# Two transformer blocks on one core: the one-hot matrix OJ of the expert gates made by GpSimd instead of VectorE

## The chip, the cores and the metric

One of the eight cores of a Trainium2 chip runs the whole program. The metric is the device time of one execution in microseconds. The engines are TensorE (PE, the matmuls, with its weight loads PEld), VectorE (DVE), ScalarE (ACT), GpSimd (POOL) and SyncE (SP, which only issues DMAs here). Each has its own queue of instructions in order, and they are tied together by semaphores.

## What is computed

Two blocks on 256 tokens of width 2048, in float32. The first has stick-breaking and dilated attention and a convolutional feed-forward part; the second has a recurrent and a gating group, and then the part on which the change bears, a mixture over 16384 experts in 128 x 128 (`peer`):

```
q = (x @ w_q).reshape(B, S, 8, 2, 128)
s = einsum('bshpk,hpnk->bshpn', q, sub_keys)
top_s, top_i = top_k(s, 16)
cand_s = top_s[..., 0, :, None] + top_s[..., 1, None, :]
cand_i = top_i[..., 0, :, None] * 128 + top_i[..., 1, None, :]
best_s, pos = top_k(cand_s, 16)          # for each head
ids, g = cand_i[pos], softmax(best_s)
out[t] = sum over the token's 8 * 16 picks of gelu(x[t] . expert_u[id]) * g * expert_v[id]
```

So each token picks 128 experts (8 heads times 16), each with an index i = id / 128, an index j = id mod 128 and a weight g.

## The kernel before

All of the program is written out engine by engine, with hand-placed waits. Every matrix of weights comes as tiles of 1 MB into three buffers `raw` (line 254), in pieces of 128 x 512. ACT rounds two pieces at a time to `hiR` (line 266), DVE subtracts that from `raw` into `loR` (line 274, the "split"; nine of these in one stage are POOL's), and PE multiplies with both, so that the sum has nearly full precision. A ring of eight pieces lies between them, and ACT and DVE work four pieces ahead (`LA`). One step `s` is one piece.

For 224 of the 256 tokens (`TD`) the mixture is computed densely. The experts are taken in three ranges of the index i (43, 43 and 42). In each range, a stage U multiplies x by all expert rows of U (`wide`, lines 292 and 293; 4 steps for each i; the sum of the two halves on DVE in line 1349, gelu in line 1357, into `S_`), and a stage V multiplies the gated result by the rows of V (`experts_out`, lines 1406 and 1408). The remaining 32 tokens (`TS`) are done by gathering their rows of U and V: POOL issues an indirect DMA (line 1447) into two buffers `ring`, and DVE takes each row into a dot product (line 1469) or a sum (line 1476). `SLOT` gives the steps at which that happens: every ten steps in stages U of the ranges 1 and 2, and every 3.5 steps in the stages V.

During each stage U the gate matrix G[j, i, t] is made: the sum of the weights g of token t over picks with these j and i. Four tokens are one gate, 56 gates for 224 tokens, `gate_at` gives the step of each: every 2 steps in range 0, every 2.8 and 2.7 in ranges 1 and 2. With the 128 picks of a token on the partitions, DVE builds three tiles in f16, each in two buffers by the parity of the gate:

- OJ (128 x 4 x 128), one where the pick's j equals the column: in range 0 with the four tokens innermost (line 1286), in the other ranges with the tokens outermost (line 1290). Both read `selb[:, 1]` (the j of each pick, f16) and the iota table `ioh4`.
- OI (128 x 4 x ni), the same for i (line 1294).
- OG, OI times the high and the low half of g (line 1297).

PE multiplies OJ (stationary) with OG (moving), eight matmuls for each gate (line 1311), two steps behind DVE. ACT brings the result to `G_` one step later (line 1320). DVE's gate k waits until PE has done gate k - 2 (semaphore `g_mm`), PE waits for `g_og` (two increments a gate) and for the bank (`g_ev`). In stage U, DVE's order within a step is: split, choice of experts or sum of V, sum of U (line 1349), gate, gathered row. POOL's program in these stages holds the gathers alone (`pool_rows`), and `selb` is made ahead of range 0 by ACT (lines 1126 and 1127) and DVE (line 1262).

Of the kernel before, what the change touches and what calls it, by code (L numbers as in the profile page):

```python
# [7 lines left out]
F16 = mybir.dt.float16  # L8
# [4 lines left out]
D = 2048  # L13
T = 256
# [99 lines left out]
def build(nc, A, out):  # L114
# [86 lines left out]
    OI = [at(f"OI{i}", o + 2 + 0.375 * i, [128, 4, NI], F16) for i in range(2)]  # L201
    OG = [at(f"OG{i}", o + 2.75 + 0.6875 * i, [128, 2, 4, NI], F16) for i in range(2)]
    o = RB + 2 * SG + 4.125
    selb = at("selb", o, [128, 4, T], F16)
    ioh4 = at("ioh4", 73, [128, 128, 4], F16)
    hrep, vsum = at("hrep", o + 2.25, [128, D]), at("vsum", o + 2.25, [128, D])
    yT = [at("yT0", 8, [128, 8, TD]), at("yT1", o + 10.25, [128, 8, TD])]
    idx = at("idx", 15, [128, ROWS, 2], U32)
    gs = at("gs", 15.25, [128, ROWS])
    dots = at("dots", 15.375, [128, ROWS, 2])  # L210
# [108 lines left out]

    norm_tmp = [tmp0, tmp1, tmp2, tmp3]  # L320
    norm_gain = [gp, g2, g4, g5]
    norm_load = [("gp", 16), ("g2", 16), ("ffn_const", 32), ("g5", 16)]
    norm_to = [XA, XA, XB, XA]
    norm_rs = [st[:, 4:6], st[:, 36:38], st[:, 68:70], st[:, 100:102]]

# [49 lines left out]
    def pe_norm_first(e, i, b):  # L375
        pe_keep(e, i, 0, b)
        if i == 0:
            e.wait_ge(S("ident"), 16)
        for q in range(TURN_FIRST[i]):
            pe_norm_turn(e, i, q)  # L380
        pe_keep(e, i, 1, b)
# [722 lines left out]
    def act_choice(e, s):  # L1104
        c, d = divmod(s - 4, 4)
        if s in (4, 7):
            c, d = 0, 7 - s
        if d == 0 and 0 <= c < 16:
            e.wait_ge(S("piece"), P_Q + (4 * c + 4 if c else 7))
            e.copy(qT[c][:, :], bank[c % 4][:, 0:T]).then_inc(S("qT"), 1)  # L1110
        h, d = divmod(s - TK0, TKP)
        if d == 1 and 0 <= h < 8:
            for tb in range(2):
                e.wait_ge(S("tk_sc"), 2 * h + tb + 1)
                if h:
                    e.wait_ge(S("tk"), TKN * (h - 1) + 20)
                e.copy(sc[tb][:, :, :].rearrange("p a b -> p (a b)"), bank[4 + tb][:, 0:T]).then_inc(S("tk_cp"), 1)
        for n, tb in enumerate((1, 0)):
            d = s - (DEC0 + DECP * n)
            if d == 8:  # L1120
                e.wait_ge(S("dec"), ND * n + 25)
                e.activation(fl[6][:, :], fl[6][:, :], ACT.Exp).then_inc(S("d_exp"), 1)
            elif d == 14:
                e.wait_ge(S("d_tr"), n + 1)
                for i in range(2):
                    e.copy(selb[:, i, half(tb)], bank[4][:, i * 128:(i + 1) * 128]).then_inc(S("sel_g"), 1)
                e.mul(selb[:, 2, half(tb)], bank[4][:, 256:384], 4096.0).then_inc(S("sel_g"), 1)

    def dve_choice(e, s):
        lo8, hi8 = slice(0, 8), slice(8, 16)  # L1130
# [52 lines left out]
        for n, tb in enumerate((1, 0)):  # L1183
# [48 lines left out]
            elif d in (3, 6):  # L1232
                w = 14 if d == 3 else 21
                for i, m in enumerate((8, 4, 2, 1)):
                    e.wait_ge(S("dec"), ND * n + w - 1 + i)
                    to = eq[:, 0:m, :, :] if m > 1 else by_rank_out(I_ if d == 3 else J_)
                    e.tensor_tensor(to, eq[:, 0:m, :, :], eq[:, m:2 * m, :, :], ALU.add).then_inc(S("dec"), 1)
            elif d == 7:
                e.tensor_tensor(v2(e1), bv, bv[:, :, 0:1].to_broadcast([128, 8, 16]), ALU.subtract).then_inc(S("dec"), 1)
            elif d == 9:  # L1240
                e.wait_ge(S("d_exp"), n + 1)
                e.reduce_sum(sm, v2(e1), AX.X).then_inc(S("dec"), 1)
                e.wait_ge(S("dec"), ND * n + 26)
                e.reciprocal(rc, sm).then_inc(S("dec"), 1)
                e.wait_ge(S("dec"), ND * n + 27)
                e.tensor_tensor(v2(g_), v2(e1), rc.unsqueeze(2).to_broadcast([128, 8, 16]), ALU.mult).then_inc(S("dec"), 1)
            elif d == 10 and n == 0:
                own, ids = slice(TD - 128, 128), xi
                e.wait_ge(S("dec"), ND)
                e.scalar_tensor_tensor(ids[own, :], I_[own, :], 128.0, J_[own, :], ALU.mult, ALU.add).then_inc(  # L1250
                    S("sp_ix"), 1)
                e.wait_ge(S("sp_ix"), 1)
                e.tensor_scalar(ids[own, :], ids[own, :], 2.0, None, ALU.mult).then_inc(S("sp_ix"), 1)
                e.wait_ge(S("sp_ix"), 2)
                for j in range(128 // TS):
                    part, cs = slice(TS * j, TS * j + TS), slice(ROWS * j, ROWS * j + ROWS)
                    e.tensor_copy(idx[part, :, 0], ids[own, cs]).then_inc(S("sp_ix"), 1)
                    e.tensor_scalar(idx[part, :, 1], ids[own, cs], 1.0, None, ALU.add).then_inc(S("sp_ix"), 1)
                    e.tensor_copy(gs[part, :], g_[own, cs]).then_inc(S("sp_ix"), 1)
            elif d == 14:  # L1260
                e.wait_ge(S("sel_g"), 3 * n + 3)
                e.scalar_tensor_tensor(selb[:, 3, half(tb)], bank[4][:, 256:384], 4096.0, selb[:, 2, half(tb)],
                                       ALU.mult, ALU.subtract).then_inc(S("sel"), 1)


# [8 lines left out]
    def dve_gates(e, r, s):  # L1274
        i0, i1 = RANGES[r]
        ni = i1 - i0
        for n in gate_at(r, s):
# [4 lines left out]
                e.wait_ge(S("choice_const"), 48)  # L1282
            if k >= 2:
                e.wait_ge(S("g_mm"), k - 1)
            if r == 0:
                e.tensor_tensor(OJ[v][:, :].rearrange("p (a t) -> p a t", t=4),
                                selb[:, 1:2, ts].to_broadcast([128, 128, 4]), ioh4[:, :, :], ALU.is_equal).then_inc(
                    S("g_og"), 1)
            else:
                e.tensor_tensor(OJ[v][:, :].rearrange("p (t a) -> p t a", t=4),  # L1290
                                selb[:, 1, ts].unsqueeze(2).to_broadcast([128, 4, 128]),
                                ioh4[:, :, 0].unsqueeze(1).to_broadcast([128, 4, 128]), ALU.is_equal).then_inc(
                    S("g_og"), 1)
# [3 lines left out]
            e.tensor_tensor(OG[v][:, :, :, 0:ni], OI[v][:, None, :, 0:ni].to_broadcast([128, 2, 4, ni]),
                            selb[:, 2:4, ts].unsqueeze(3).to_broadcast([128, 2, 4, ni]), ALU.mult).then_inc(
                S("g_og"), 1)

    def pe_gates(e, r, s):
        ni = RANGES[r][1] - RANGES[r][0]
        for n in gate_at(r, s - 2):
            k, v, b = NG * r + n, n % 2, u_bank(r) + 2 + n % 2
            e.wait_ge(S("g_og"), 2 * k + 2)
            if n >= 2:
                e.wait_ge(S("g_ev"), k - 1)
            for j in range(4):
                of = slice(j, 512, 4) if r == 0 else slice(128 * j, 128 * j + 128)
                for w in range(2):  # L1310
                    m = e.matmul(bank[b][:, ni * j:ni * j + ni], OJ[v][:, of], OG[v][:, w, j, 0:ni], start=(w == 0),  # L1311
                                 stop=(w == 1))
# [137 lines left out]

    def act_rows(e, s):
        if SLOT.get(s - 1) == NROW:
            e.wait_ge(S("sp_dot"), 1)
            e.activation(gated[:, :], gated[:, :], ACT.Gelu_apprx_tanh).then_inc(S("sp_gelu"), 1)

    def dve_rows(e, s):
        if SLOT.get(s - 2) == NROW:
            e.wait_ge(S("sp_gelu"), 1)
            e.wait_ge(S("sp_ix"), 2 + 3 * (128 // TS))
            e.tensor_tensor(gated[:, :], gated[:, :], gs[:, :], ALU.mult).then_inc(S("sp_a"), 1)  # L1460
        m = row_of(s)
        if m is not None:
            e.wait_ge(S(f"row{m % 2}"), 16 * (m // 2 + 1))
# [5 lines left out]
                e.scalar_tensor_tensor(rg, rg, 1.0, hrep[:, cs], ALU.mult, ALU.mult,  # L1469
                                       accum_out=dots[:, j, m % 2:m % 2 + 1]).then_inc(S("sp_use"), 1)  # L1470
            elif j == 0:
                e.wait_ge(S("sp_a"), 1)
                e.tensor_scalar(vsum[:, cs], rg, gated[:, 0:1], None, ALU.mult).then_inc(S("sp_use"), 1)
            else:
                e.wait_ge(S("sp_use"), m - 1)
# [1 line left out]
                    S("sp_use"), 1)  # L1477
        if SLOT.get(s) == NROW:
            e.wait_ge(S("sp_use"), NROW)
            e.tensor_tensor(gated[:, :], dots[:, :, 0], dots[:, :, 1], ALU.add).then_inc(S("sp_dot"), 1)  # L1480

# [242 lines left out]
    def act_program(e):  # L1726
# [1 line left out]
        e.wait_ge(S("cst"), 2)  # L1728
        act_sqrt_table(e, 0)
        e.wait_ge(S("x0"), 16)  # L1730
        e.activation(tmp0[:, 0, :], x[:, 0, :], ACT.Square, accum_out=ss[:, 0:1]).then_inc(S("x0sq"), 1)
        e.wait_ge(S("x0sq"), 1)
        e.wait_ge(S("x1sq"), 1)
        act_root(e, 0, ss)
        act_norm_hi(e, 0, 0)
        split_hi(e, 0)
# [136 lines left out]
    def dve_program(e):  # L1873
# [3 lines left out]
        e.memset(warm[:, :], 0.0).then_inc(S("cst"), 1)  # L1877
        e.wait_ge(S("x1"), 16)
        e.scalar_tensor_tensor(tmp0[:, 1, :], x[:, 1, :], 1.0, x[:, 1, :], ALU.mult, ALU.mult,
                               accum_out=ss[:, 1:2]).then_inc(S("x1sq"), 1)  # L1880
        dve_root(e, 0, ss)
        dve_norm_scale(e, 0, 0)
        dve_norm_scale(e, 0, 1)
# [163 lines left out]
    def pool_program(e):  # L2047
# [207 lines left out]
```

## Time and profile before

| | |
|---|---|
| median of 3 runs | 2960.62 us (2955.79 to 2963.03) |
| the profiled execution | 2955.81 us, of which the span of instructions is 2954.5 us |
| mean granted clock of PE | 0.997 |
| PE busy | 2911.7 us (99%), 18502 matmuls |
| DVE busy | 2139.5 us (72%) |
| ACT busy | 1570.7 us (53%) |
| POOL busy | 419.0 us (14%), 304 instructions |
| splits on DVE (line 274) | 1255.0 us |
| read from memory | 623 MB, 212 GB/s over the span |

Busy shares are means over the whole span; which engine sets the pace has to be read stage by stage. A row of PE has a modelled end, so that matmuls overlap in the rows: the distance between starts says more than the duration. Idle time on an engine that is not the limit costs nothing.

### The profile page before, as it was taken

Reading aid. Unit: us, or ns where it says so; the run is one execution under the profiler, and the core shown is the slowest. Engines: PE = TensorE matmul, PEld = TensorE weight load, DVE = VectorE, ACT = ScalarE, POOL = GpSimd, SP = SyncE. Lnnn points to the kernel's source line nnn. Section 1 sums busy time; section 2 is a strip of 40 time slices with the busy share of each in tenths; the row PEclk is TensorE's granted clock in tenths of the full one; section 3 lists DMA queues with packets and bytes.
Section 4 is the critical chain, followed back from the end, with each engine's and each line's share of the span. In section 5 each row is a group of like instructions: output and inputs, shape, how many; then the busy total and the mean of one; then the engine's idle time right before and its main releaser. Section 6 shows DMA issues by size and latency. Waiting matters only on the chain.

```text
span 2954.5 us, 45739 instructions
## 1 busy us (share of the span) xinstructions
PE 2911.7 (99%) x18502; PEld 2631.0 (89%) x18502; DVE 2139.5 (72%) x3352; ACT 1570.7 (53%) x2406; POOL 419.0 (14%) x304
## 2 busy tenths in 40 slices
PE   9999999999999999999998999999999999999998
PEld 7888888888888888899898999999999999999997
DVE  5566566666666455676589889778999777999776
ACT  4467755555555443577444556444556444556534
POOL 0011101111111000143020000232010133110131
PEclk9999999999999999999999999999999999999999
DMA  7544445555556554654564555788666788666784
GB/s 259 177 151 152 156 177 186 185 186 187 185 186 222 190 198 143 221 177 170 208 211 171 190 183 203 270 302 298 230 236 227 247 306 302 234 232 239 272 310 168
DMA packets 99009, 631.53 MB, mean 214 GB/s; under 512 B 11376, under 2 KB 12784, under 8 KB 31216
## 3 DMA queue, kind: packets, MB, share of 16 engines
q1 hardware_dynamic: 80368, 561.49, 54.3%
q0 software_dynamic: 18432, 67.12, 6.3%
q8 instruction: 148, 2.42, 0.3%
q14 instruction: 61, 0.50, 0.0%
HBM read 623.32 MB, written 4.19 MB: 212 GB/s over the span
## 4 chain that ended last, share of the span: by engine, by line
PE 78%; DMA 9%; DVE 8%; ACT 3%; issue 2%; SPq 0%; ACTq 0%; DVEq 0%
PE ps L292 26%; PE ps L293 13%; PE ps L1406 6%; PE ps L314 6%; PE ps L316 6%; PE ps L315 6%; DMA ring<-in_u_rows_dram,idx 5%; DMA ring<-in_v_rows_dram,idx 4%; PE ps L1408 3%; DVE loR L274 3%; PE ps L305 2%; PE ps L304 2%; PE ps L303 2%; ACT hiR L266 1%; PE ps L1311 1%
## 5 line engine op out<-in xcount | busy, mean ns | idle before, releaser
L274 DVE TENSOR_TENSOR loR<-raw,hiR 128x1024 fp32r<-128x1024 f32 x1017 | 1255.0, 1241 | 621.9 <-ACT hiR L266 618.4
L266 ACT CAST hiR<-raw 128x1024 fp32r<-128x1024 f32 x1026 | 1074.4, 1051 | 803.3 <-PE ps L1408 324.3
L292 PE MATMUL ps<-XA,hiR 128*128 128x448 f32 (+1 forms) x3936 | 1343.9, 391 | 10.7 <-DVE loR L274 9.3
L293 PE MATMUL ps<-XA,loR 128*128 128x224 f32 (+1 forms) x3936 | 1069.3, 272 | 0.0
L292 PEld LDWEIGHTS ps<-XA,hiR 128*128 128x128 f32 x3936 | 739.7, 188 | 127.1 <-DVE loR L274 6.6
L293 PEld LDWEIGHTS ps<-XA,loR 128*128 128x128 f32 x3936 | 747.7, 190 | 0.6
L1406 PE MATMUL ps<-hl,hiR 128*128 128x448 f32 x2048 | 651.0, 377 | 6.2 <-DVE loR L274 5.9
L1408 PE MATMUL ps<-hl,loR 128*128 128x224 f32 x2048 | 543.5, 265 | 0.0
L1406 PEld LDWEIGHTS ps<-hl,hiR 128*128 128x128 f32 x2048 | 385.2, 188 | 42.8 <-DVE loR L274 9.2
L1408 PEld LDWEIGHTS ps<-hl,loR 128*128 128x128 f32 x2048 | 392.1, 191 | 0.2 <-issue 0.2
L1447 POOL DMA_INDIRECT ring<-in_u_rows_dram,idx x64 | 103.2, 1612 | 716.8 <-DVE ring L1469 664.8
L1320 ACT ACTIVATE G__147<-ps 128x172 f32<-128x172 f32 (+1 forms) x168 | 52.9, 315 | 227.8 <-PE ps L1311 227.7
L1447 POOL DMA_INDIRECT ring<-in_v_rows_dram,idx x64 | 105.2, 1644 | 407.9 <-DVE vsum L1476 391.8
L314 PE MATMUL ps<-hiR,Y 128*128 128x512 f32 x344 | 133.8, 389 | 0.0
L315 PE MATMUL ps<-loR,Y 128*128 128x512 f32 x344 | 133.8, 389 | 0.0
L316 PE MATMUL ps<-hiR,Y 128*128 128x512 f32 x344 | 133.8, 389 | 0.0
L1469 DVE SCALAR_TENSOR_TENSOR ring<-ring,hrep 128x1024 f32<-128x1024 f32 x64 | 78.2, 1222 | 54.6 <-DMA ring<-in_u_rows_dram,idx 54.5
L1476 DVE SCALAR_TENSOR_TENSOR vsum<-ring,gated,vsum 128x1024 f32<-128x1024 f32 x62 | 79.5, 1282 | 47.5 <-DMA ring<-in_v_rows_dram,idx 47.4
L303 PE MATMUL ps<-XB,hiR 128*128 128x256 f32 x384 | 110.0, 286 | 0.0
L305 PE MATMUL ps<-XB,loR 128*128 128x256 f32 x384 | 108.6, 283 | 0.0
L304 PE MATMUL ps<-XB,hiR 128*128 128x256 f32 x384 | 108.6, 283 | 0.0
L314 PE MATMUL ps<-hiR,XA 128*128 128x512 f32 x256 | 101.0, 394 | 2.3 <-DVE loR L274 1.8
(307 smaller groups left out, 3490.1 us busy)
## 6 DMA issues: line engine op xcount, KB each, us to landing
raw<-in_u_dram SPq DMA_DIRECT2D x128, 1024.0 KB
raw<-in_v_dram SPq DMA_DIRECT2D x128, 1024.0 KB
raw<-in_w_up_dram SPq DMA_DIRECT2D x86, 1024.0 KB
raw<-in_w_down_dram SPq DMA_DIRECT2D x43, 1024.0 KB
raw<-in_w_in_qk_dram SPq DMA_DIRECT2D x32, 1024.0 KB
raw<-in_w_out_dram SPq DMA_DIRECT2D x32, 1024.0 KB
raw<-in_w_in_dram SPq DMA_DIRECT2D x24, 1024.0 KB
raw<-in_w_in_v_dram SPq DMA_DIRECT2D x16, 1024.0 KB
```

The lines of the kernel that those rows point to most:

```text
L266: e.copy(hiR[:, r:r + 2, :], raw[n % NR][:, q:q + 2, :]).then_inc(S("hi"), 1)
L274: e.tensor_tensor(loR[:, r:r + 2, :], raw[n % NR][:, q:q + 2, :], hiR[:, r:r + 2, :].bitcast(F32), ALU.subtract).then_inc(S("lo_pool" if p ...
L292: e.matmul(both, wh, X.hl[:, :, k, 0:nt], start=(k == 0), stop=False, skip_group_check=True)
L293: m = e.matmul(dst[:, 0:nt], wl, X.h[:, k, 0:nt], start=False, stop=(k == KC - 1), skip_group_check=True)
L303: e.matmul(dst, wh, X.h[:, k, :], start=(k == 0), stop=False)
L304: e.matmul(dst, wh, X.l[:, k, :], start=False, stop=False)
L314: e.matmul(dsts[tb], ah_, hi, start=first, stop=False)
L315: e.matmul(dsts[tb], ah_, lo, start=False, stop=False)
L316: m = e.matmul(dsts[tb], al_, hi, start=False, stop=last)
L1406: e.matmul(b[:, 0:2 * TD].rearrange("p (a t) -> p a t", a=2), wh, hl[:, :, i, :], start=(i == 0), stop=False, skip_group_check=True)
L1408: m = e.matmul(b[:, 0:TD], wl, hl[:, 0, i, :], start=False, stop=(i == i1 - i0 - 1), skip_group_check=True)
L1447: e.indirect_dma_start(ring[m % 2][:, :], None, A["u_rows" if m < NROW else "v_rows"], bass.IndirectOffsetOnAxis(ap=idx[:, m % NROW // 2, ...
```

## The change

OJ is no longer made by DVE. POOL makes it in all ranges with the tokens outermost, with four comparisons (one for each token, 128 columns) of the iota with a scalar for each partition, one step ahead of DVE's OI and OG. For this the j of each pick is kept as a float32 tile `jf` instead of a part of `selb`, PE waits for a new semaphore `g_oj`, and in range 0 too its stationary operand is contiguous. POOL's program now goes through the ranges, with the gates of a step ahead of the gathers of that step. To free semaphores, `ident` shares that of the first gain, the two sums of squares at the start share one, and three semaphores of the gathered tokens become one. The handling of the 32 gathered tokens is as it was.

```diff
-    selb = at("selb", o, [128, 4, T], F16)
+    selb, jf = at("selb", o, [128, 3, T], F16), at("jf", o + 1.5, [128, T])
...
-    norm_load = [("gp", 16), ("g2", 16), ("ffn_const", 32), ("g5", 16)]
+    norm_load = [("gp", 32), ("g2", 16), ("ffn_const", 32), ("g5", 16)]
...
-            e.wait_ge(S("ident"), 16)
+            e.wait_ge(S("gp"), 32)
...
-                for i in range(2):
-                    e.copy(selb[:, i, half(tb)], bank[4][:, i * 128:(i + 1) * 128]).then_inc(S("sel_g"), 1)
-                e.mul(selb[:, 2, half(tb)], bank[4][:, 256:384], 4096.0).then_inc(S("sel_g"), 1)
+                e.copy(selb[:, 0, half(tb)], bank[4][:, 0:128]).then_inc(S("sel_g"), 1)
+                e.copy(jf[:, half(tb)], bank[4][:, 128:256]).then_inc(S("sel_g"), 1)
+                e.mul(selb[:, 1, half(tb)], bank[4][:, 256:384], 4096.0).then_inc(S("sel_g"), 1)
...
-            if r == 0:
-                e.tensor_tensor(OJ[v][:, :].rearrange("p (a t) -> p a t", t=4),
-                                selb[:, 1:2, ts].to_broadcast([128, 128, 4]), ioh4[:, :, :], ALU.is_equal).then_inc(
-                    S("g_og"), 1)
-            else:
-                e.tensor_tensor(OJ[v][:, :].rearrange("p (t a) -> p t a", t=4),
-                                selb[:, 1, ts].unsqueeze(2).to_broadcast([128, 4, 128]),
-                                ioh4[:, :, 0].unsqueeze(1).to_broadcast([128, 4, 128]), ALU.is_equal).then_inc(
-                    S("g_og"), 1)
...
+    def pool_gates(e, r, s):
+        for n in gate_at(r, s + 1):
+            k, v = NG * r + n, n % 2
+            if k == 0:
+                e.wait_ge(S("sel"), 2)
+                e.wait_ge(S("choice_const"), 48)
+            if k >= 2:
+                e.wait_ge(S("g_mm"), k - 1)
+            for j in range(4):
+                m = e.tensor_scalar(OJ[v][:, 128 * j:128 * j + 128], ioh4[:, :, 0], jf[:, 4 * n + j:4 * n + j + 1], None,
+                                    ALU.is_equal)
+            m.then_inc(S("g_oj"), 1)
...
-            e.wait_ge(S("g_og"), 2 * k + 2)
+            e.wait_ge(S("g_oj"), k + 1)
+            e.wait_ge(S("g_og"), k + 1)
...
-                of = slice(j, 512, 4) if r == 0 else slice(128 * j, 128 * j + 128)
+                of = slice(128 * j, 128 * j + 128)
...
-        for s in range(P_VV[2] + 4 * (RANGES[2][1] - RANGES[2][0]) - P_U[0]):
-            pool_rows(e, s)
+        for r, (i0, i1) in enumerate(RANGES):
+            for s in range(4 * (i1 - i0)):
+                pool_gates(e, r, s)
+                pool_rows(e, P_U[r] - P_U[0] + s)
+            for s in range(4 * (i1 - i0)):
+                pool_rows(e, P_VV[r] - P_U[0] + s)
...
-        load(e, "ident", ident[:, :], A["ident"])
+        load(e, "gp", ident[:, :], A["ident"])
```

## Rows read from the trace of the kernel before

**Rows 1.** Busy by stretch: start:end, length, then PE, PEld, DVE, ACT, POOL (instructions); clock, DMA.
```profile
1639.50:1800.00 160.50, 160.50 (x1344) 148.47 (x1343) 138.43 (x253) 83.91 (x166) 0.00 (x0) 1.00 0.54 186
...
2040.00:2243.00 203.00, 201.31 (x1608) 186.94 (x1607) 190.59 (x304) 109.50 (x200) 22.02 (x15) 1.00 0.69 236
...
2500.00:2702.00 202.00, 202.00 (x1634) 187.90 (x1633) 191.35 (x292) 110.33 (x203) 22.62 (x15) 1.00 0.68 233
```

**Rows 2.** PE's waits, 1800 to 2050 us: total, times, longest.
```profile
PE ps L1406 <- DVE loR L274: 2.5, 4, 1.1
PE ps L1311 <- DVE OG L1297: 1.2, 1, 1.2
```

**Rows 3.** Line 1311 by stretch: length, then PE and PEld busy.
```profile
1640.00:1800.00 160.00, 24.65 (x448) 19.23 (x448) 1.00 0.54 185
...
2500.00:2700.00 200.00, 20.34 (x440) 14.55 (x440) 1.00 0.69 234
```

**Rows 4.** Line 1311's weight loads in these two stretches: ns min/median/max, first and last start.
```profile
L1311 PEld LDWEIGHTS ps<-OG,OJ x448: 111/118/129, 1641.7 to 1799.9; 128*128 128x128 f16 x150
...
L1311 PEld LDWEIGHTS ps<-OG,OJ x440: 95/96/100, 2499.9 to 2697.9; 128*128 128x128 f16 x147
```

**Rows 5.** Timeline of PE at one gate of range 0 and of range 1: start, duration.
```profile
1730.66 0.26 PE L293 MATMUL ps<-XA,loR 128*128 128x224 f32 x1
...
1730.77 0.44 PE L1311 MATMUL ps<-OG,OJ 128*128 128x43 f16 x8
...
1731.05 0.45 PE L292 MATMUL ps<-XA,hiR 128*128 128x448 f32 x1
...
2161.35 0.37 PE L1311 MATMUL ps<-OG,OJ 128*128 128x43 f16 x8
...
2161.56 0.45 PE L292 MATMUL ps<-XA,hiR 128*128 128x448 f32 x1
```

**Rows 6.** The comparisons for OJ on DVE, by line: ns min/median/max.
```profile
L1286 DVE TENSOR_TENSOR OJ<-selb,ioh x56: 417/419/421, 1639.5 to 1796.9; 128x512 f16<-128x512 f16 x56
...
L1290 DVE TENSOR_TENSOR OJ<-selb,ioh x112: 682/685/692, 2042.0 to 2697.7; 128x512 f16<-128x512 f16 x112
```

**Rows 7.** Elementwise instructions on POOL, by line: ns min/median/max.
```profile
L837 POOL TENSOR_TENSOR acc<-acc,acc x43: 732/739/744, 467.3 to 941.4; 128x256 f32<-128x256 f32 x43
...
L755 POOL TENSOR_TENSOR tdl<-tdl,tdl x8: 1296/1304/2330, 124.9 to 322.1; 128x512 f32<-128x512 f32 x8
```

**Rows 8.** Timelines of POOL and of DVE, at 1246 and at 468 us.
```profile
1246.18 0.74 POOL L1014 TENSOR_TENSOR gm<-gm,guT 128x256 f32<-128x256 f32 x1 [8.41 <-DVE gm L985]
...
1246.18 1.81 DVE L274 TENSOR_TENSOR loR<-raw,hiR 128x1024 fp32r<-128x1024 f32 x1
...
468.58 1.16 POOL L841 TENSOR_TENSOR Y<-acc,Y 128x256 fp32r<-128x256 f32 x1 [0.52 <-ACT Y L814]
...
467.75 1.39 DVE L274 TENSOR_TENSOR loR<-raw,hiR 128x1024 fp32r<-128x1024 f32 x1 [0.58 <-ACT hiR L266]
```

**Rows 9.** Timelines of DVE and PE between two gates of range 0.
```profile
1729.66 1.23 DVE L274 TENSOR_TENSOR loR<-raw,hiR 128x1024 fp32r<-128x1024 f32 x1 [0.51 <-ACT hiR L266]
...
1731.44 0.33 DVE L1294 TENSOR_TENSOR OI<-selb,ioh 128x172 f16<-128x172 f16 x1
1731.80 0.52 DVE L1297 TENSOR_TENSOR OG<-OI,selb 128x344 f16<-128x344 f16 x1
...
1733.64 0.44 PE L1311 MATMUL ps<-OG,OJ 128*128 128x43 f16 x8
```

**Rows 10.** DVE's dot products with gathered rows: ns min/median/max, first and last start.
```profile
L1469 DVE SCALAR_TENSOR_TENSOR ring<-ring,hrep x64: 1217/1221/1227, 1875.2 to 2381.5; 128x1024 f32<-128x1024 f32 x64
```

**Rows 11.** The start: issue of ident, its landing time in the DMA list, the first norm step.
```profile
2.12 0.68 SPq L2067 DMA_DIRECT2D ident<-in_ident_dram  x1
...
ident<-in_ident_dram SPq DMA_DIRECT2D x1, 64.0 KB, 8.8
...
11.12 2.74 DVE L335 SCALAR_TENSOR_TENSOR tmpx<-x,st,gp 128x512 f32<-128x512 f32 x4
```

More of the change, by code:

```diff
@@ L203, in build @@
     o = RB + 2 * SG + 4.125
-    selb = at("selb", o, [128, 4, T], F16)
+    selb, jf = at("selb", o, [128, 3, T], F16), at("jf", o + 1.5, [128, T])
     ioh4 = at("ioh4", 73, [128, 128, 4], F16)
-    hrep, vsum = at("hrep", o + 2.25, [128, D]), at("vsum", o + 2.25, [128, D])
-    yT = [at("yT0", 8, [128, 8, TD]), at("yT1", o + 10.25, [128, 8, TD])]
+    hrep, vsum = at("hrep", o + 2.5, [128, D]), at("vsum", o + 2.5, [128, D])
+    yT = [at("yT0", 8, [128, 8, TD]), at("yT1", o + 10.5, [128, 8, TD])]
     idx = at("idx", 15, [128, ROWS, 2], U32)
@@ L1261, in dve_choice @@
                 e.wait_ge(S("sel_g"), 3 * n + 3)
-                e.scalar_tensor_tensor(selb[:, 3, half(tb)], bank[4][:, 256:384], 4096.0, selb[:, 2, half(tb)],
+                e.scalar_tensor_tensor(selb[:, 2, half(tb)], bank[4][:, 256:384], 4096.0, selb[:, 1, half(tb)],
                                        ALU.mult, ALU.subtract).then_inc(S("sel"), 1)
@@ L1297, in dve_gates @@
             e.tensor_tensor(OG[v][:, :, :, 0:ni], OI[v][:, None, :, 0:ni].to_broadcast([128, 2, 4, ni]),
[L1298 removed]
+                            selb[:, 1:3, ts].unsqueeze(3).to_broadcast([128, 2, 4, ni]), ALU.mult).then_inc(
                 S("g_og"), 1)
+    def pool_gates(e, r, s):
[10 more added lines that the diff above has]
+            m.then_inc(S("g_oj"), 1)
     def pe_gates(e, r, s):
@@ L1452, in act_rows @@
         if SLOT.get(s - 1) == NROW:
-            e.wait_ge(S("sp_dot"), 1)
-            e.activation(gated[:, :], gated[:, :], ACT.Gelu_apprx_tanh).then_inc(S("sp_gelu"), 1)
+            e.wait_ge(S("sp_g"), 1)
+            e.activation(gated[:, :], gated[:, :], ACT.Gelu_apprx_tanh).then_inc(S("sp_g"), 1)
     def dve_rows(e, s):
         if SLOT.get(s - 2) == NROW:
-            e.wait_ge(S("sp_gelu"), 1)
+            e.wait_ge(S("sp_g"), 2)
             e.wait_ge(S("sp_ix"), 2 + 3 * (128 // TS))
-            e.tensor_tensor(gated[:, :], gated[:, :], gs[:, :], ALU.mult).then_inc(S("sp_a"), 1)
+            e.tensor_tensor(gated[:, :], gated[:, :], gs[:, :], ALU.mult).then_inc(S("sp_g"), 1)
         m = row_of(s)
@@ L1471, in dve_rows @@
             elif j == 0:
-                e.wait_ge(S("sp_a"), 1)
+                e.wait_ge(S("sp_g"), 3)
                 e.tensor_scalar(vsum[:, cs], rg, gated[:, 0:1], None, ALU.mult).then_inc(S("sp_use"), 1)
@@ L1479, in dve_rows @@
             e.wait_ge(S("sp_use"), NROW)
-            e.tensor_tensor(gated[:, :], dots[:, :, 0], dots[:, :, 1], ALU.add).then_inc(S("sp_dot"), 1)
+            e.tensor_tensor(gated[:, :], dots[:, :, 0], dots[:, :, 1], ALU.add).then_inc(S("sp_g"), 1)
     Y_AT = [NI - 1 + 26 + (NI - 1) * f for f in range(3)]
@@ L1730, in act_program @@
         e.wait_ge(S("x0"), 16)
-        e.activation(tmp0[:, 0, :], x[:, 0, :], ACT.Square, accum_out=ss[:, 0:1]).then_inc(S("x0sq"), 1)
-        e.wait_ge(S("x0sq"), 1)
-        e.wait_ge(S("x1sq"), 1)
+        e.activation(tmp0[:, 0, :], x[:, 0, :], ACT.Square, accum_out=ss[:, 0:1]).then_inc(S("xsq"), 1)
+        e.wait_ge(S("xsq"), 2)
         act_root(e, 0, ss)
@@ L1879, in dve_program @@
         e.scalar_tensor_tensor(tmp0[:, 1, :], x[:, 1, :], 1.0, x[:, 1, :], ALU.mult, ALU.mult,
-                               accum_out=ss[:, 1:2]).then_inc(S("x1sq"), 1)
+                               accum_out=ss[:, 1:2]).then_inc(S("xsq"), 1)
         dve_root(e, 0, ss)
```

## The prediction

> **What bounds the kernel now.** The first view to read is the busy time by stretch, because the change touches only three stretches, those in which the gate matrices are made. In the three of them TensorE (PE) is busy for 160.5 of 160.5 us, 201.3 of 203 us and 202.0 of 202 us, at a granted clock of 1.00 (its upper level, 2.4 GHz), while VectorE (DVE) is busy for 138.4, 190.6 and 191.4 us and GpSimd (POOL) for 0, 22 and 23 us [rows 1]. So PE sets the pace, DVE is close behind it (86, 94 and 95%), and POOL is nearly free. The second view is what PE waits for. In the stretch of the first range there is no wait at all; the only wait for a gate matrix is one of 1.2 us at the start of the second range, and the other waits there are for weight splits in the stage that multiplies by V, 2.5 us in four waits [rows 2]. A change that only takes work from DVE can therefore win back almost nothing here: DVE's work lies beneath PE's. What can move the time is what PE itself does, or an engine that gets later than PE.
>
> **Part 1: PE's own work, the one sure gain.** Before, the first range keeps OJ with the four tokens interleaved, so that PE loads its stationary operand with a step of four f16 elements (8 bytes); the other ranges load it contiguous. The change makes all ranges contiguous. PE's time in line 1311 is 24.65 us for 448 matmuls (56 gates) with the step and 20.34 us for 440 (55 gates) without: 0.440 and 0.370 us for a gate [rows 3]. The loads show it: 118 ns against 96 ns [rows 4]. And it is on the path, since the next weight matmul begins 0.28 us after the block does with the step and 0.21 us without, in a queue with no idle time [rows 5]. Each gate of the first range gives 0.07 us: 56 x 0.07 = 3.9 us off. The third range's tile is one column narrower per token (42 for 43); the timeline pair of rows 5 is from the second range, with 43, and gives the same 0.07, so the width is not what makes the difference. Bounds: 0 (if something other than the step made it) to 4.2 us (0.075 x 56).
> The Trainium skill, "SBUF — State Buffer" (the note on cachelines below the port swizzle), says that two or more accesses for each line of 16 bytes keep full speed, which a step of 8 bytes just meets. By that the step costs nothing, this term is 0, and the sum below would be 2955.2 instead of 2951.3; the 118 ns beside 96 ns speak against it, so the row decides.
>
> **Part 2: DVE loses 168 comparisons.** 56 of 0.42 us and 112 of 0.685 us [rows 6]: 23.5 and 76.7 us, 100 us in all. All of it is covered by PE today except where PE waits for the gate matrix, at the start of the second range: 1.2 us [rows 2]. There OJ of 0.685 us stands directly ahead of OI and OG on DVE, so the wait shrinks by 0.6 us (0 to 1.2). What is next to end it is OG itself. I take 0.6.
>
> **Part 3: POOL gains 672 comparisons of 128 columns (four for each of 168 gates).** No row shows this operation on POOL. The nearest are its two-input additions and multiplications: 0.74 us for 256 columns and 1.30 us for 512 [rows 7], which is 0.56 us for 256 more columns, so 0.18 us fixed and 2.2 ns for a column. With 128 columns and two inputs that is 0.18 + 0.28 = 0.46 us; if one input costs half of the streaming it is 0.32 us. I take 0.32 to 0.46 us and, the new form reading one tile only, 0.38, so 1.5 us for a gate. As a bound above I keep the whole 0.74 us, below 0.18 us. A gate comes every 160.5/56 = 2.87 us in the first range (2.80 after part 1) and every 203/56 = 3.6 us in the others [rows 1]. OJ has two buffers: POOL may start one as soon as PE is done with the gate before last, so it has two gate intervals, 5.6 us, for 1.5 us of work. Latency is no problem; what counts is whether POOL gets through in one interval, and what it does to DVE.
> They do meet. At 1246 us, long before the gates, a POOL multiplication of 256 columns begins with DVE's split, and that split takes 1.81 us where it takes 1.23 us alone: 0.58 us lost, the streaming part of POOL's operation. The other way round, a POOL operation that starts inside a split takes 1.16 us instead of 0.74, and ends 0.60 us after the split does [rows 7 to 9]. So each holds the other off. Scaled to 128 columns, one comparison can hold DVE by 0.14 to 0.31 us; I take 0.2. For a gate DVE has three instructions with two SBUF inputs (split, OI, OG), which I count as the ones that can be held, once each: 3 x 0.2 = 0.6 us (0 to 0.93). DVE's work for a gate in the first range is 138.4/56 = 2.47 us; without OJ's 0.42 it is 2.05, with 0.6 it is 2.65 against PE's 2.80. In the others 190.6/56 = 3.40, less 0.69, plus 0.6 to 0.8 (the work on gathered rows is held too) makes 3.3 to 3.5 against 3.6. So DVE ends about as loaded as it was, and it stays covered, if barely. Its gate tile was ready 1.3 us before PE took it: OG ends at 1732.32 and PE's block starts at 1733.64 [rows 9]. Without OJ there are 1.7 us, into which the 0.6 fits. POOL for a gate: 4 x 0.38 = 1.5 us and at most the 1.6 us for which DVE's three instructions stream (1.23, 0.33 and 0.52 us [rows 9], less 0.15 each, as the split streams only after it), of which 3 x 0.14 lies over POOL's fixed part: 2.7 us against 2.80. Cost taken: nothing; the bounds are in the rivals.
> The rule that speaks against this change is in the Trainium skill, "SBUF — State Buffer", the section on the shared port pair: a DVE instruction with two SBUF inputs and a GpSimd instruction that reads SBUF exclude each other for the whole instruction. The rows just read agree. Its "GPSIMD Engine Reference" (sections 3.1 and 7) puts a one-input body at 1.03 to 1.9 cycles of 1.2 GHz for a column; an estimate from that page is 0.11 to 0.20 us of streaming, the lower half of my span.
>
> **Part 4: waits and queue order.** PE now waits for g_oj and g_og instead of g_og alone. Behind that wait stand all later weight matmuls, so a late OJ costs its full lateness. The instruction itself I take at zero (at most the 0.11 us named next for each of 168, 18 us, if it could not be fetched ahead): PE's block starts 0.11 us after the start of the matmul ahead of it [rows 5], with a wait for g_og and one for g_ev between them, and no gap is to be seen. On POOL, OJ of each step now stands ahead of that step's gathers. In ranges 1 and 2 one gather comes every ten steps, some 12 us, with two buffers, so 2 us later issue is covered. The first two gathers move from before the first range's gates to behind them, about 1800, still 75 us ahead of their first use at 1875.2 [rows 10]. At the start, the norm's first step on DVE and PE's transposes now wait for gain and ident together: ident is issued at 2.12 and lands 8.8 us after, at 10.9, and DVE needs it at 11.12 [rows 11]. No cost; 0.7 us if landing counts from the end of the issue. jf is written by one ACT copy in place of one, the joined semaphores replace others: nothing.
>
> **Sum.** The profiled execution took 2955.8 us (span 2954.5 and 1.3 around it). 2955.8 - 3.9 - 0.6 = 2951.3. The median of the runs shown is 2960.6, 4.8 above it; against the median the same saving of 4.5 gives 2956.1, and that is my number.
>
> **Rivals.**
> B, slower: the port between POOL and DVE decides. Place: the gate stretches of all ranges. If a comparison costs 0.46 us and holds DVE by 0.31, POOL needs 4 x 0.46 + 1.6 - 0.4 = 3.0 us, up to 3.4 if nothing overlaps, against 2.80: 0.2 to 0.6, say 0.4 x 56 = 22 us; in the others DVE comes to 3.40 - 0.69 + 1.0 = 3.7 against 3.6, some 0.14 x 112 = 16 us. Together +38, less 4.5: 2955.8 + 33 = 2989 (2994 by the median). It decides from a comparison of about 0.40 us on. For it: the holding rows. Against it: one input in place of two.
> C, much slower: the comparison on POOL is as slow as the 256-column row, 0.74 us. POOL then needs 2.96 + 1.2 = 4.15 us for a gate: (4.15 - 2.80) x 56 + (4.15 - 3.6) x 112 = 76 + 62 = 138 us, less 4.5: 3089 us. Against it: nothing in the rows makes half the columns cost as much.
> D, the strided load isn't what costs the 0.07 us, or the added wait costs it again: 2955.2 us, 2960 by the median.
> E, faster: DVE's earlier finish also takes away waits for splits just past the gate stretches; 2.5 us in four waits in the one shown [rows 2], and as an estimate as much again behind the next range: 4 to 5 us more, 2946.5, 2951 by the median. Against it: those lie in stages whose DVE queue stands behind the gathers.
>
> **How the numbers follow.** Forecast A 0.62, D 0.08, E 0.07, B 0.17, C 0.06. A's own range is 2948 to 2963 (the runs of the kernel before spread over 7 us). The range for 8 in 10 takes in D, E and the lower half of B, and leaves C and the rest of B out: 2947 to 2982. This kernel's measurement tells about 0.3%, 9 us, from no change. A's 4.5 us lies within it, as does D; E and the edge of A give faster 0.09; B and C give slower 0.23; same is 0.68.
>
> **What would show it.** PE in line 1311 of the first range (with its new number) at 0.37 us for a gate and loads at 96 ns; no wait of PE for POOL's OJ; DVE busy down by less than 100 us, since some splits lengthen by 0.1 to 0.3 us beside POOL; POOL busy up by 672 x 0.38, some 255 us, more where it is held. The forecast is wrong if PE's waits list OJ on POOL or splits within the gate stretches, or if the first range's stretch gets longer than 160 us.

## The result, and the profile after

The changed kernel takes 3042.5 us (median, 3041.0 to 3044.4), 1.0288 of the kernel before (95% interval 1.0269 to 1.0306). That is 84 us slower where 4.5 us faster was forecast, and it lies 60 us above the range. The profiled execution has a span of 3040.4 us.

The waits of PE in the changed kernel, longest in total first (total us, times, longest):

```profile
PE ps L1316 <- POOL OJ L1301: 70.7, 94, 2.2
PE ps L292 <- DVE loR L274: 9.4, 11, 1.8
PE ps L1411 <- DVE loR L274: 6.9, 9, 1.5
...
PE ps L1316 <- DVE OG L1288: 1.3, 1, 1.3
```

The first row is new; in the kernel before, the only wait of this kind was for OG [rows 2], and that one is still there. The rest of the 86 us shows as 15.0 us more of busy time for the same 18502 matmuls (2926.7 in place of 2911.7 us), whose ends are modelled. The groups of the page and the forms on POOL show what a comparison costs:

```profile
L1301 POOL TENSOR_SCALAR OJ<-ioh,jf 128x128 f16<-128x128 f16 x672 | 620.4, 939 | 82.7 <-DVE selb L1262 80.0 <-PE ps L1316 1.5
```

A comparison takes 0.94 us where 0.38 was assumed, so 3.76 us a gate. Before it POOL idled 80 us for the first gate's input and 1.5 us for PE in all: from the first gate to the last it is never done early. The busy times by stretch say the same (start:end, length, then PE, PEld, DVE, ACT, POOL; clock, DMA); they answer to rows 1:

```profile
1634.00:1850.00 216.00, 189.83 (x1502) 168.15 (x1501) 150.55 (x241) 102.57 (x204) 196.31 (x226) 1.00 0.49 168
...
2066.00:2328.00 262.00, 239.67 (x1831) 220.19 (x1830) 198.30 (x297) 128.87 (x238) 239.33 (x241) 0.99 0.62 212
2548.00:2805.00 257.00, 232.86 (x1791) 212.78 (x1790) 191.61 (x275) 125.67 (x232) 232.12 (x240) 0.99 0.61 207
```

In the two later ranges POOL is busy for 91 and 90% of the stretch, in the first nearly all of the time from the first gate on, and PE, which had no gaps, now has some. DVE, from 94% before, is down to 76 and 75%. The bound has moved from PE to POOL, and the relief of DVE bought nothing here.

Where the 86 us of the span arose, by the start of each stage in PE's timeline (first matmul of line 292, or of line 1406, which is 1411 after):

```
stage                 before   after   difference
up to U of range 0    1565.2   1563.1    -2.1
U, range 0             251.2    281.9   +30.7
V, range 0             220.8    221.4    +0.6
U, range 1             234.3    261.2   +26.9
V, range 1             223.4    220.1    -3.3
U, range 2             227.2    257.5   +30.3
V, range 2, and end    232.4    235.1    +2.7
```

All of it lies in the three stages with gates. The gates in range 0, every 2.87 us before, come every 3.43 us, and the ones shown wait for OJ, as 94 of all 168 do (PE's timeline in the changed kernel, start and duration):

```profile
1643.04 0.37 PE L1316 MATMUL ps<-OG,OJ 128*128 128x43 f16 x8 [0.49 <-POOL OJ L1301]
...
1646.45 0.37 PE L1316 MATMUL ps<-OG,OJ 128*128 128x43 f16 x8 [0.45 <-POOL OJ L1301]
...
1649.89 0.37 PE L1316 MATMUL ps<-OG,OJ 128*128 128x43 f16 x8 [0.49 <-POOL OJ L1301]
```

### The profile page after: what moved, and what is told of

Same layout as the page of the kernel before. It is cut to its first block, busy times and chain, and to the rows that moved or that the text cites. A ratio compares the mean times of both kernels' runs of the same rounds, so it can differ in the third digit from the quotient of the medians.

```text
span 3040.4 us, 46249 instructions
## 1 busy us (share of the span) xinstructions
PE 2926.7 (96%) x18502; PEld 2629.5 (86%) x18502; DVE 2087.0 (69%) x3184; ACT 1567.2 (52%) x2406; POOL 1033.7 (34%) x976
## 4 chain that ended last, share of the span: by engine, by line
PE 57%; POOL 21%; DMA 9%; DVE 6%; ACT 3%; issue 2%; SPq 0%; ACTq 0%; DVEq 0%
POOL OJ L1301 20%; PE ps L292 14%; PE ps L293 7%; PE ps L1411 6%; PE ps L314 6%; PE ps L316 6%; PE ps L315 6%; DMA ring<-in_u_rows_dram,idx 4%; DMA ring<-in_v_rows_dram,idx 4%; PE ps L1413 3%; PE ps L305 2%; PE ps L304 2%; PE ps L303 2%; DVE loR L274 2%; POOL ring L1452 1%
## 5 line engine op out<-in xcount | busy, mean ns | idle before, releaser
L1301 POOL TENSOR_SCALAR OJ<-ioh,jf 128x128 f16<-128x128 f16 x672 | 620.4, 939 | 82.7 <-DVE selb L1262 80.0
L837 POOL TENSOR_TENSOR acc<-acc,acc 128x256 f32<-128x256 f32 x43 | 31.7, 737 | 475.6 <-DVE acc L791 475.6
L1316 PEld LDWEIGHTS ps<-OG,OJ 128*128 128x128 f16 x1344 | 44.7, 96 | 107.8 <-POOL OJ L1301 100.8
L1316 PE MATMUL ps<-OG,OJ 128*128 128x43 f16 (+1 forms) x1344 | 62.4, 183 | 72.6 <-POOL OJ L1301 70.7
```

The lines of the kernel that those rows point to most:

```text
L1301: m = e.tensor_scalar(OJ[v][:, 128 * j:128 * j + 128], ioh4[:, :, 0], jf[:, 4 * n + j:4 * n + j + 1], None, ALU.is_equal)
```

## The experiments

**Theories.** T, throughput: POOL can't make four comparisons in the time in which PE comes to the next gate; the rest of the change is sound. Its rival W: the loss comes from the new order of waits and queues, or from POOL holding DVE off, whatever a comparison lasts. Within T there are three causes for the 0.94 us: F, a cost of each instruction; C, a cost of each column (or of the step of 8 bytes); H, DVE holding POOL off.

**1. The contiguous operand by itself.** OJ stays with DVE; only range 0 gets the layout of the others.

```diff
-            if r == 0:
-                e.tensor_tensor(OJ[v][:, :].rearrange("p (a t) -> p a t", t=4), ...
-            else:
-                e.tensor_tensor(OJ[v][:, :].rearrange("p (t a) -> p t a", t=4), ...
+            e.tensor_tensor(OJ[v][:, :].rearrange("p (t a) -> p t a", t=4), ...
...
-                of = slice(j, 512, 4) if r == 0 else slice(128 * j, 128 * j + 128)
+                of = slice(128 * j, 128 * j + 128)
```

> The kernel before, with OJ of the first range laid out with the tokens outermost too (the form that the other ranges have), still made by DVE; nothing of the rest of the change. If the step of four elements is what costs PE 0.07 us a gate, line 1311 takes 0.37 us a gate in the first range in place of 0.44, and the time falls by 3.9 us (ratio 0.9987). If it is something else in that range, the ratio is 1.000. DVE's comparison rises from 0.42 to 0.685 us, 15 us over the stretch, which takes DVE from 86% to about 95% busy there: if that is too much, PE waits for OG and the time rises by up to 15 us.

Measured: 2954.6 us, ratio 0.9988 (0.9976 to 1.0001). The whole run alone can't tell that from nothing, but the stage can: U of range 0 takes 247.3 us in place of 251.2, exactly 3.9 less. Line 1311 (1306 here) in a stretch of range 0, PE and PEld busy, and its weight loads:

```profile
1638.00:1798.00 160.00, 20.78 (x448) 14.89 (x448) 1.00 0.56 191
...
L1306 PEld LDWEIGHTS ps<-OG,OJ x448: 95/96/100, 1639.9 to 1794.2; 128*128 128x128 f16 x150
```

20.78 us for 56 gates in place of 24.65, loads at 96 ns in place of 118 [rows 3, 4]. So the step costs what part 1 of the prediction said. DVE was busy for 153.5 of 160.5 us there (96%) and PE still had no wait in it.

**2. Half the dose.** DVE makes OJ of two of the four tokens, POOL that of the other two.

```diff
+            e.tensor_tensor(OJ[v][:, 0:256].rearrange("p (t a) -> p t a", t=2),
+                            jf[:, 4 * n:4 * n + 2].unsqueeze(2).to_broadcast([128, 2, 128]),
+                            ioh4[:, :, 0].unsqueeze(1).to_broadcast([128, 2, 128]), ALU.is_equal).then_inc(
+                S("g_og"), 1)
...
-            for j in range(4):
+            for j in (2, 3):
...
-            e.wait_ge(S("g_og"), k + 1)
+            e.wait_ge(S("g_og"), 2 * k + 2)
```

> The changed kernel with half the dose: DVE makes OJ of two of a gate's four tokens with one comparison of 256 columns, POOL the other two with two comparisons. If POOL's throughput (0.9 us for each comparison against 2.80 us a gate) is the whole cause, two of them need 1.8 us, PE waits for no OJ, and the time is 2951 to 2956 us, 0.9975 to 0.9995 of the kernel before. If the loss comes from somewhere else (the added wait on PE, the order of POOL's queue, or POOL holding DVE off), half or more of the 86 us stays: 2990 to 3040 us.

Measured: 2952.1 us, ratio 0.9985 (0.9974 to 0.9996). It leaves nothing out, and it is faster than both kernels, by a little. Its comparisons are no faster:

```profile
L1305 POOL TENSOR_SCALAR OJ<-ioh,jf 128x128 f16<-128x128 f16 x336 | 311.7, 939 | 226.2 <-PE ps L1320 145.2 <-DVE selb L1262 80.1
```

But there are two for a gate, 1.9 us, and POOL now waits 145 us for PE to free the buffer. No wait of PE for OJ is left, with the same wait on `g_oj`, the same order of POOL's queue and the same contiguous tile. W falls, T stands. (Half as many comparisons also hold DVE off half as much; experiments 3 and 7, with all of OJ on POOL, have no wait for OJ either.) U of range 0 takes 247.3 us, as in experiment 1, so the gain in that stage is that of the operand and of nothing else.

**3. One comparison of 512 columns.**

```diff
-            for j in range(4):
-                m = e.tensor_scalar(OJ[v][:, 128 * j:128 * j + 128], ioh4[:, :, 0], jf[:, 4 * n + j:4 * n + j + 1], None,
-                                    ALU.is_equal)
+            m = e.tensor_scalar(OJ[v][:, :].rearrange("p (t a) -> p t a", t=4),
+                                ioh4[:, :, 0].unsqueeze(1).to_broadcast([128, 4, 128]), jf[:, 4 * n:4 * n + 1], None,
+                                ALU.is_equal)
```

> The changed kernel with one comparison of 512 columns for a gate on POOL in place of four of 128 (the scalar of the gate's first token is used for all four tokens, so the gate matrices are those of other picks; the amount of data is the same). Theory F, a fixed cost of each POOL instruction: four times 0.92 us become some 0.5 + 0.44 us, POOL falls to about 1 us a gate, PE's waits for OJ go and the time is 2951 to 2958 us. Theory C, a cost for each column (step of 8 bytes, f16): one instruction takes about 2.4 us or more, and together with DVE's holding POOL still needs nearly 3 us a gate: 2980 to 3040 us.

Measured: 2949.5 us, ratio 0.9978 (0.9964 to 0.9992).

```profile
L1300 POOL TENSOR_SCALAR OJ<-ioh,jf 128x512 f16<-128x512 f16 x168 | 317.0, 1889 | 218.0 <-PE ps L1316 136.5 <-DVE selb L1262 80.1
```

1.89 us for a gate in place of 3.76, with the same columns: half of the cost goes with the number of instructions. But neither F nor C is right by itself, since 1.89 is nearly twice what F gave and less than what C gave.

**4. The comparison by itself.** Before all else, with no DVE instruction running, POOL does rows of measuring instructions; then four comparisons beside six DVE additions that read SBUF twice, and four beside six DVE sums that read it once.

```diff
+        for _ in range(4):
+            e.tensor_scalar(mo[:, o, :], m16[:, 0:128], sc, None, ALU.is_equal).then_inc(mb, 1)
+            o += 1
+        for _ in range(4):
+            e.tensor_scalar(mo[:, o, :], s4, sc, None, ALU.is_equal).then_inc(mb, 1)
+            o += 1
...
+        for i in range(6):
+            e.tensor_tensor(m6[:, i, :], m32[:, :], m32[:, :], ALU.add).then_inc(S("md_"), 1)
...
+        for i in range(6):
+            e.reduce_sum(md[:, 4 + i:5 + i], m32[:, :], AX.X).then_inc(S("md_"), 1)
```

> The changed kernel with a piece of measuring work ahead of it, in which no DVE instruction runs beside POOL: comparisons of 128 f16 columns with a scalar from a tile, packed and with a step of 8 bytes; with a constant; of 512 columns; of 128 float32 columns; additions of 128 columns in float32 and f16. Then four strided comparisons beside DVE additions with two SBUF inputs, and four beside DVE sums with one. The time means nothing here. Theory F (fixed cost): all comparisons of 128 columns take 0.55 to 0.65 us whatever the step and type, 512 columns 0.9 to 1.1 us. Theory C (columns): the packed ones take under 0.4 us, 512 columns four times as long. Theory H (DVE holds POOL off): alone 0.6 us from start to start, beside two-input additions near one per DVE instruction, some 1.2 us, beside one-input sums again 0.6 us.

By line, ns min/median/max: packed, step of 8 bytes, against a constant, 512 columns, float32, and the two-input additions in float32 and in f16:

```profile
L2081 POOL TENSOR_SCALAR mo<-m,m x4: 590/595/609, 2.2 to 4.0; 128x128 f16<-128x128 f16 x4
...
L2084 POOL TENSOR_SCALAR mo<-m,m x4: 595/599/607, 4.6 to 6.3; 128x128 f16<-128x128 f16 x4
...
L2087 POOL TENSOR_SCALAR mo<-m x3: 516/516/517, 6.9 to 7.9; 128x128 f16<-128x128 f16 x3
...
L2090 POOL TENSOR_SCALAR mo<-m,m x2: 1551/1551/1551, 8.4 to 10.0; 128x512 f16<-128x512 f16 x2
...
L2094 POOL TENSOR_SCALAR mf<-m x3: 590/590/591, 11.5 to 12.7; 128x128 f32<-128x128 f32 x3
...
L2096 POOL TENSOR_TENSOR mf<-m x3: 442/442/443, 13.2 to 14.0; 128x128 f32<-128x128 f32 x3
...
L2098 POOL TENSOR_TENSOR mo<-m x3: 414/414/414, 14.4 to 15.2; 128x128 f16<-128x128 f16 x3
```

From 128 to 512 columns there are 0.96 us, 2.5 ns for a column, which leaves 0.27 us for the instruction. Step and type do nothing, the scalar from a tile costs 0.08 us over a constant. The addition of two tiles, 0.44 us, is what the prediction had scaled from its rows (0.46); the comparison with a single input is dearer than that, by 0.15 us. Then the timelines of POOL and DVE beside each other (a row x4 merges four; the first two of the held four are also given singly):

```profile
15.85 2.57 POOL L2103 TENSOR_SCALAR mo<-m,m 128x128 f16<-128x128 f16 x1 [0.23 <-DVE md L1891]
...
18.40 2.39 POOL L2103 TENSOR_SCALAR mo<-m,m 128x128 f16<-128x128 f16 x1
...
15.85 7.89 POOL L2103 TENSOR_SCALAR mo<-m,m 128x128 f16<-128x128 f16 x4 [0.23 <-DVE md L1891]
24.04 2.36 POOL L2103 TENSOR_SCALAR mo<-m,m 128x128 f16<-128x128 f16 x4 [0.30 <-DVE md L1896]
...
15.67 1.22 DVE L1893 TENSOR_TENSOR m<-m 128x1024 f32<-128x1024 f32 x1 [14.62 <-issue]
...
16.81 5.96 DVE L1893 TENSOR_TENSOR m<-m 128x1024 f32<-128x1024 f32 x5
```

Beside two-input additions four comparisons take 7.89 us, beside one-input sums 2.36, the 0.59 us each that they take alone. DVE's six additions ended at 22.77, 7.1 us after they began, where six at their spacing of 1.14 us are 6.9: DVE loses 0.2 us, POOL 5.5. Theory H had the sign right and the size too small: each of the first three comparisons (2.57, 2.39 and 2.39 us) is passed by two additions, not by one, and the fourth, begun after the last addition, takes 0.60 us. The Trainium skill, "SBUF — State Buffer", the section "Who interferes with whom", says that an instruction of DVE with two SBUF inputs and one of POOL that reads SBUF exclude each other for the whole instruction, and that a DVE instruction with one input doesn't contend. The second half agrees with the 2.36 us. Of the first, these rows show POOL's side alone: the three comparisons that were let through cost DVE 0.2 us in all, far less than they last.

**5. The holding taken away in the whole kernel.** The splits of the three U stages read one tile; the comparisons stay.

```diff
+        if any(P_U[a] <= g < P_VV[a] for a in range(3)):
+            c = 232 + g // 2 % 8
+            e.tensor_scalar(loR[:, r:r + 2, :], raw[n % NR][:, q:q + 2, :], 1.0, None, ALU.mult, ALU.add,
+                            accum_out=st[:, c:c + 1]).then_inc(S("lo_dve"), 1)
+            return
```

> The changed kernel, in which DVE's splits of the three U stages read one tile in SBUF in place of two (loR gets the whole of raw instead of raw - hiR, a multiplication by 1 with a sum written out as well, so that those stages count the high part twice); POOL's comparisons and everything else stay. Theory H (a DVE instruction with two SBUF inputs holds POOL off, and that is what lifts a comparison from 0.60 us alone to 0.92 us): without the splits a comparison falls to 0.65 to 0.75 us, a gate on POOL to 2.6 to 3.0 us, and 50 to 86 of the 86 us go: 2950 to 2990 us. Theory F alone (the comparison's own length is enough, DVE doesn't matter): a comparison stays at 0.9 us and the time at 3040 us.

Measured: 2949.0 us, ratio 0.9976 (0.9965 to 0.9987). The splits last as long as ever (1.216 us), POOL does all 672 comparisons, and these fall to 0.65 us:

```profile
L1306 POOL TENSOR_SCALAR OJ<-ioh,jf 128x128 f16<-128x128 f16 x672 | 423.6, 646 | 147.2 <-DVE selb L1267 80.1 <-PE ps L1321 62.9
```

With 2.6 us a gate POOL is inside PE's 2.80, waits 63 us for PE, and all of the loss is gone. So the length of the comparison alone would have done no harm: 4 x 0.595 = 2.38 us fits. It takes DVE's splits on top.

**6. A comparison that is 0.08 us shorter.**

```diff
-                m = e.tensor_scalar(..., ioh4[:, :, 0], jf[:, 4 * n + j:4 * n + j + 1], None,
+                m = e.tensor_scalar(..., ioh4[:, :, 0], 3.0, None,
```

> The changed kernel with each of the four comparisons against a constant in place of the scalar in jf (so that OJ marks the picks of no token; the work is the same but for reading the scalar). Alone that takes 0.516 us in place of 0.595, 0.08 us less. If POOL's throughput sets the pace in all three gate stretches, the time falls by 4 x 0.08 x 168 = 53 us, to about 2989 us, ratio 1.011. If PE waits for something that doesn't depend on the length of the comparison, it stays at 3040 us.

Measured: 2957.1 us, ratio 1.0002 (0.9990 to 1.0013). (Each row of OJ marks column 3 here.) Not 53 but 85 us went, so the expectation, in which a gate gets shorter by the comparisons' own 0.08 us each and by nothing else, was wrong. PE still has five waits for OJ, 4.2 us in all. The timeline of single instructions on POOL, with DVE's and PE's beside it, shows why:

```profile
1649.67 0.53 POOL L1301 TENSOR_SCALAR OJ<-ioh 128x128 f16<-128x128 f16 x1
1650.18 1.27 POOL L1301 TENSOR_SCALAR OJ<-ioh 128x128 f16<-128x128 f16 x1
1651.42 0.53 POOL L1301 TENSOR_SCALAR OJ<-ioh 128x128 f16<-128x128 f16 x1
1651.92 0.56 POOL L1301 TENSOR_SCALAR OJ<-ioh 128x128 f16<-128x128 f16 x1
...
1649.79 1.26 DVE L274 TENSOR_TENSOR loR<-raw,hiR 128x1024 fp32r<-128x1024 f32 x1 [0.48 <-ACT hiR L266]
...
1650.90 0.37 PE L1316 MATMUL ps<-OG,OJ 128*128 128x43 f16 x8
...
1653.70 0.37 PE L1316 MATMUL ps<-OG,OJ 128*128 128x43 f16 x8
```

The holding comes with the split, in range 0 once for a gate: the comparison that meets it takes 1.27 us, 0.75 more, the others 0.53 to 0.58. A gate on POOL is 4 x 0.516 + 0.75 = 2.81 us, just PE's 2.80 (1650.90 to 1653.70). In the changed kernel the same picture has a heavier hit:

```profile
1650.41 0.63 POOL L1301 TENSOR_SCALAR OJ<-ioh,jf 128x128 f16<-128x128 f16 x1
1651.01 0.61 POOL L1301 TENSOR_SCALAR OJ<-ioh,jf 128x128 f16<-128x128 f16 x1
1651.60 1.64 POOL L1301 TENSOR_SCALAR OJ<-ioh,jf 128x128 f16<-128x128 f16 x1
...
1651.59 1.27 DVE L274 TENSOR_TENSOR loR<-raw,hiR 128x1024 fp32r<-128x1024 f32 x1 [1.02 <-ACT hiR L266]
```

There 1.64 us is 1.04 above the 0.60 of the others, and a gate is 2.4 + 1.0 = 3.4 us, the 3.43 measured. That POOL is right at the point where it decides is why 0.08 us a comparison give back nearly everything: 0.32 us of the 0.6 a gate are the comparisons' own, 0.3 the smaller hit. In both pictures the held comparison ends 0.4 us after the split does (1651.45 and 1651.05 here, 1653.24 and 1652.86 there), but here it begins 0.39 us after the split's start and there 0.01 us: that is the difference between the hits. Why the two engines fall into these steps isn't shown. Over the changed kernel's three gate stages 58, 77 and 76 comparisons take 1.2 us or more, beside 57, 80 and 77 splits, so the long ones are about as many as the splits.

**7. Two comparisons of 256 columns.**

```diff
-            for j in range(4):
+            for j in (0, 2):
...
+                                    ioh4[:, :, 0].unsqueeze(1).to_broadcast([128, 2, 128]),
```

> The changed kernel with two comparisons of 256 columns for a gate in place of four of 128 (each with the scalar of its first token, so half of the tokens get another token's OJ; the amount of data is the same). From the runs so far a comparison alone is 0.27 us plus 2.5 ns for a column, and DVE adds about 0.3 us to each instruction, whatever its length: 2 x (0.27 + 0.64 + 0.3) = 2.4 us a gate, under PE's 2.80, so no wait for OJ and 2950 to 2956 us, ratio 0.998. If the columns mattered more than the number of instructions, 3000 us or more.

Measured: 2950.8 us, ratio 0.9977 (0.9964 to 0.9990); the comparison takes 1.43 us in the mean, 2.86 a gate over all ranges, and PE waits for no OJ. The time came as expected, the length of the comparison didn't (1.2 expected), as the holding goes with the splits. So the right time was partly luck: in the gates of range 0 POOL has no idle time left and only just keeps up.

**8. The iota table packed.**

```diff
-    ioh4 = at("ioh4", 73, [128, 128, 4], F16)
+    ioh4 = at("ioh4", 73, [128, 4, 128], F16)
...
-    c["iota_h"] = np.repeat(np.arange(128, dtype=np.float16), 4)
+    c["iota_h"] = np.tile(np.arange(128, dtype=np.float16), 4)
```

> The changed kernel with the iota table laid out packed, so that POOL (and DVE for OI) reads it with a step of 2 bytes in place of 8. The comparisons alone took 0.590 us packed and 0.595 with the step, so nothing should change: 3035 to 3045 us. If the step mattered beside DVE, the time would fall by tens of us.

Measured: 3039.9 us, ratio 1.0275 (1.0250 to 1.0299), with 0.936 us for a comparison. As expected, the step of 8 bytes is no part of it.

## Why the prediction was wrong, step by step

**What bounds the kernel** was read rightly: PE without a gap and DVE hidden beneath it. Taking 100 us of comparisons from DVE won nothing in the changed kernel. Where POOL isn't late it may be worth a little: the three runs in which DVE makes no OJ and PE doesn't wait for it (experiments 3, 5 and 7) stand at 0.9976 to 0.9978, 1 and 2 at 0.9988 and 0.9985, and U of range 1 takes 232.2 to 232.7 us in the former, 235.0 and 234.0 in the latter. The intervals overlap, so these 2 to 3 us are not shown.

**Part 1, the strided operand** held to the tenth: 3.9 us predicted, 3.9 us in U of range 0 in experiments 1 and 2, 96 ns for a load. The rule of the Trainium skill, "SBUF — State Buffer", that two accesses for each line of 16 bytes keep full speed doesn't hold for this load: 118 ns with the step, 96 without. In the changed kernel the gain is there and buried.

**Part 2, 0.6 us at the start of the second range**, didn't come: PE's wait for OG is 1.3 us where it was 1.2. In the profiles of experiments 3, 6, 7 and 8, in which POOL makes all of OJ too, the wait there is 0 to 0.3 us, and in experiment 1, where DVE makes it all, 1.9. So the direction was right, and why the changed kernel keeps 1.3 is open.

**Part 3 is the step that failed, in its first term.** A comparison was priced at 0.38 us, on the grounds that one input must be cheaper than two. The two-input figure scaled from rows 7 was good (0.46, measured 0.44). The inference from the number of inputs was not: 0.595 us. It was outside even the 0.32 to 0.46 from which the value was taken, though inside the outer bound of 0.74. The second term, 1.6 - 0.4 = 1.2 us of holding by DVE, was about right against 1.0 measured, though by luck in its make-up: it counted three DVE instructions, and of these only the split holds POOL by much. In range 0 the comparisons that meet OG alone take 0.68 us in the mean and those that meet no DVE instruction 0.61. Put the measured price into the prediction's own sum and it gives 4 x 0.595 + 1.2 = 3.6 us for a gate against 2.80, and 45 us for range 0. Measured is 3.43 and, counting what part 1 gave, 30.7 + 3.9 = 34.6 us. The time lost was in the sum, and it stood 0.1 us below the threshold (2.7 against 2.80) with a price that no row showed.

In the later ranges rival B had put only DVE's load in question, and the sum for POOL left the gathers out, though they stand in the same queue. The interval was misread too: the stretch of 203 us holds 53 gates, not 56, and the gates before come every 3.82 us in range 1 and 3.67 in range 2 (first to last: 2043.6 to 2253.7 and 2499.9 to 2701.7), not every 3.6. POOL needs 3.8 us for the comparisons of a gate (186.2 us for 195 comparisons between 2090 and 2300), which is just PE's interval; on top there are 17 gathers of 1.45 us in the mean between the first and the last gate of range 1, and 16 of 1.33 in range 2, 25 and 21 us beside the 26.9 and 30.3 us lost. By this sum the gathers are most of the loss there; no run took them away.

**Part 3, what POOL does to DVE**, was overpriced. OG rose from 0.517 to 0.594 us, OI from 0.331 to 0.375 and the split from 1.226 to 1.261 in range 0: 0.16 us a gate, not 0.6. The multiplication read in rows 8 is the only one of its line's eight in which POOL began first, by 6 ns in the trace. The other seven begin 0.16 us after a split and take 1.65 us:

```profile
L1014 POOL TENSOR_TENSOR gm<-gm,guT x8: 738/1650/1656, 1246.2 to 1375.8; 128x256 f32<-128x256 f32 x8
```

So the kernel before already had seven cases in which POOL lost 0.9 us, and one in which DVE lost 0.58; in the steady state of the gates it is POOL that is held off.

**Part 4** held. The added wait on PE costs nothing (experiment 2 has it). The first norm step begins at 11.06 us, where it began at 11.12 [rows 11], so joining `ident` with the gain is free; the first two gathers are issued at 1828.5 and first used at 1903.8, with no wait of PE between that could be theirs.

**The rivals.** What happened is B's mechanism, DVE and POOL holding each other off, by way of C's cause, a comparison dearer than assumed, and the 3042.5 us lie between B's 2994 and C's 3089 (some 3093 by the median). B named its point of decision rightly (a comparison of about 0.40 us); the chance of 0.23 for both was too low for a term whose form no row showed, and the range ended where B was half way.

## What to carry to other kernels

When work moves to an engine that looked idle, that engine's time for one round has to be compared with the round of the engine that sets the pace, with everything else in its queue and with the time for which other engines' instructions hold it off; the idle share over the span doesn't show any of this. The interval is read from the first to the last instruction of the group, and a pair of rows that shows who holds off whom is checked against all others of its line. A price for an operation that no row shows must not be taken from the thought that fewer inputs are cheaper, and where the sum stands within a few per cent of the threshold, the range has to reach past it. And the gain of a bundle may lie in the smallest part: here a contiguous stationary operand, which half the dose keeps (0.9985).

## What the runs showed of the hardware that was not expected

A comparison of 128 columns with a scalar from a tile takes GpSimd 0.595 us, and some 2.5 ns for each further column (1.551 us for 512); it is dearer than an addition of two tiles (0.442 us), in f16 and in float32, packed and with a step of 8 bytes. Two-input VectorE additions of 1.2 us, one after the other, let such a comparison through only every 2.4 us and lose 0.2 us in 7 themselves, so the two engines don't share the time evenly. VectorE sums that read SBUF once don't slow the comparison at all (0.59 us). TensorE's load of a 128 x 128 stationary operand in f16 takes 118 ns with a step of 8 bytes and 96 ns without.
